# Two dense layers in split float32 on TensorE: the moving operand read as two halves in turn, one column of each

## The reference

```python
proj = h @ w_in                      # 2048 x 13312 of block one, 2048 x 6160 of block two
oa @ w_o_attn; orr @ w_o_ret; merged @ w_out
g, u = jnp.split(h2 @ w_ffn_in, 2, axis=-1)      # 2048 x 11264
x + (jax.nn.silu(g) * u) @ w_ffn_out             # 5632 x 2048
```

## Time and profile before

| | |
|---|---|
| median of 3 runs | 2798.41 us (2797.48 to 2807.46) |
| the profiled execution, its own time | 2805.7 us |
| its span | 2803.6 us |
| granted TensorE clock, mean | 0.995 |
| busy: TensorE / VectorE / ScalarE / GpSimd | 2757.4 / 1602.8 / 1309.6 / 89.6 us |
| HBM read | 504.39 MB, mean 181 GB/s |

### The profile page before, as it was taken

One profiled execution on the slowest core, in us unless ns is written; L12 is line 12 of the kernel. 1 busy time (PEld: TensorE's weight loads), 2 busy tenths in 40 slices (PEclk: granted clock), 3 DMA queues, 4 the chain that ended last, 5 costly groups with the idle time before them and its releaser, 6 DMA issues.

```text
span 2803.6 us, 37336 instructions
## 1 busy us (share of the span) xinstructions
PE 2757.4 (98%) x13344; PEld 2302.9 (82%) x13344; DVE 1602.8 (57%) x1640; ACT 1309.6 (47%) x1545; POOL 89.6 (3%) x61
## 2 busy tenths in 40 slices
PE   8999999999999999999999999998999999999998
PEld 7887778788888888888888888787788888888886
DVE  5557655545555444444454555586676666666455
ACT  5445555454445444444444444454554444444444
POOL 0000000000000000000000000021000000000000
PEclk9999999999999999999999999999999999999999
DMA  7665555566666666666666666543456666666554
GB/s 233 184 184 164 160 170 163 166 207 213 188 188 182 193 187 187 188 188 192 187 193 192 189 180 184 154 128 121 143 173 191 190 188 187 188 191 192 193 193 150
DMA packets 233286, 507.67 MB, mean 181 GB/s; under 512 B 15829, under 2 KB 18229, under 8 KB 232436
## 3 DMA queue, kind: packets, MB, share of 16 engines
q1 hardware_dynamic: 231712, 499.31, 59.6%
q0 software_dynamic: 1360, 7.21, 0.8%
q10 hardware_dynamic: 132, 0.03, 0.0%
HBM read 504.39 MB, written 2.10 MB: 181 GB/s over the span
## 4 chain that ended last, share of the span: by engine, by line
PE 94%; DVE 2%; ACT 2%; issue 1%; DMA 0%; DVEq 0%; ACTq 0%; SPq 0%
PE ps L359 20%; PE ps L361 20%; PE ps L360 20%; PE ps L349 18%; PE ps L350 10%; DVE wlo L1303 1%; PE ps L426 1%; ACT whi L841 1%; PE ps L730 1%; PE ps L722 0%; PE ps L663 0%; ACT hT L887 0%; PE ps L494 0%; PE ps L784 0%; PE ps L557 0%
## 5 line engine op out<-in xcount | busy, mean ns | idle before, releaser
L1303 DVE TENSOR_TENSOR wlo<-raw,whi 128x1024 fp32r<-128x1024 f32 x944 | 1172.3, 1243 | 1123.2 <-ACT whi L841 1115.2
L841 ACT ACTIVATE whi<-raw 128x1024 fp32r<-128x1024 f32 x944 | 999.9, 1060 | 1418.5 <-PE ps L361 991.3
L349 PE MATMUL ps<-hT,whi 128*128 128x512 f32 x2304 | 807.7, 395 | 5.8 <-DVE wlo L1303 4.2
L359 PE MATMUL ps<-whi,hT 128*128 128x512 f32 x1792 | 715.4, 399 | 7.5 <-ACT big L945 2.4
L361 PE MATMUL ps<-whi,hT 128*128 128x512 f32 x1792 | 701.7, 392 | 0.0
L360 PE MATMUL ps<-wlo,hT 128*128 128x512 f32 x1792 | 701.0, 391 | 0.0
L350 PE MATMUL ps<-hT,wlo 128*128 128x256 f32 x2304 | 645.7, 280 | 0.0
L349 PEld LDWEIGHTS ps<-hT,whi 128*128 128x128 f32 x2304 | 431.7, 187 | 106.6 <-issue 4.8
L350 PEld LDWEIGHTS ps<-hT,wlo 128*128 128x128 f32 x2304 | 435.4, 189 | 0.1
L359 PEld LDWEIGHTS ps<-whi,hT 128*128 128x128 f32 x1792 | 338.5, 189 | 80.3 <-issue 2.9
L361 PEld LDWEIGHTS ps<-whi,hT 128*128 128x128 f32 x1792 | 338.3, 189 | 71.9
(11 more groups left out here) (246 smaller groups left out, 1084.6 us busy)
## 6 DMA issues: line engine op xcount, KB each, us to landing
raw<-w_ffn_in SPq DMA_DIRECT2D x352, 512.0 KB, 3.7
raw<-w_in SPq DMA_DIRECT2D x304, 512.0 KB, 3.8
raw<-w_ffn_out SPq DMA_DIRECT2D x176, 512.0 KB, 3.6
raw<-w_o_ret SPq DMA_DIRECT2D x32, 512.0 KB, 4.7
raw<-w_out SPq DMA_DIRECT2D x32, 512.0 KB, 3.9
raw<-w_o SPq DMA_DIRECT2D x32, 512.0 KB, 3.6
raw<-w_o_attn SPq DMA_DIRECT2D x16, 512.0 KB, 4.3
resid<-x SPq DMA_DIRECT2D x8, 256.0 KB, 6.2
```

Source lines behind the costliest of these rows:

```text
L349: pe.matmul(acc, whi[:, c % SLOTS, f], hT[:, kt, :, :], start=(kt == 0), stop=False)
L359: pe.matmul(acc, hi, whi[:, c % SLOTS, f], start=start, stop=False)
L841: act.activation(whi[:, c % SLOTS, :], raw[:, c % SLOTS, :], ACT.Copy).then_inc(hi_ready, 1)
L1303: dve.tensor_tensor(wlo[:, c % SLOTS, :], raw[:, c % SLOTS, :], whi[:, c % SLOTS, :].bitcast(F32), ALU.subtract).then_inc(lo_ready, 1)
```

## The change

The numbers that are computed stay the same; only the order of columns inside a bank changes. A new helper `in_turn` reads a run of N columns as two halves of N/2 and takes one column of each in turn: 0, N/2, 1, N/2 + 1, and so on. The weight products (`cols_block` and `rows_mm`) take their moving operand in that order, so the sums lie in PSUM in that order. The matmuls still write PSUM in order. Stationary operands, the small float32 matmuls and the transposes are as before.

Every reader of those accumulators now reads PSUM in order (`as_taken` only gives the same addresses the shape of the other operand) and reads and writes its SBUF operands through `in_turn`. In `rows_mm` and in the `rows` readers the two halves of 512 columns lie 256 columns (1024 bytes) apart. In `cols_block` each 256-column part is halved by itself, so the two lie 128 columns (512 bytes) apart. No instruction, wait, buffer or transfer is added or removed.

```diff
+        def in_turn(x):
+
+            return x.rearrange("p (b a) -> p a b", b=2) if len(x.shape) == 2 else x.rearrange("p n (b a) -> p n a b", b=2)
+
+        def as_taken(acc):
+
+            return acc.rearrange("p (a b) -> p a b", b=2) if len(acc.shape) == 2 else acc.rearrange("p n (a b) -> p n a b", b=2)
...
-                            pe.matmul(acc, whi[:, c % SLOTS, f], hT[:, kt, :, :], start=(kt == 0), stop=False)
-                            mm = pe.matmul(acc[:, 0:SEQ], wlo[:, c % SLOTS, f], hT[:, kt, 0, :], start=False,
+                            pe.matmul(acc, whi[:, c % SLOTS, f], in_turn(hT[:, kt, :, :]), start=(kt == 0), stop=False)
+                            mm = pe.matmul(acc[:, 0:SEQ], wlo[:, c % SLOTS, f], in_turn(hT[:, kt, 0, :]), start=False,
                                            stop=(kt == KT - 1))
...
-                pe.matmul(acc, hi, whi[:, c % SLOTS, f], start=start, stop=False)
-                pe.matmul(acc, hi, wlo[:, c % SLOTS, f], start=False, stop=False)
-                return pe.matmul(acc, lo, whi[:, c % SLOTS, f], start=False, stop=stop)
+                w_hi, w_lo = in_turn(whi[:, c % SLOTS, f]), in_turn(wlo[:, c % SLOTS, f])
+                pe.matmul(acc, hi, w_hi, start=start, stop=False)
+                pe.matmul(acc, hi, w_lo, start=False, stop=False)
+                return pe.matmul(acc, lo, w_hi, start=False, stop=stop)
...
-                act.activation(lo_sum.rearrange("p (f t) -> p f t", f=4), ps[:, 4 * par:4 * par + 4, SEQ:], ACT.Copy)\
+                act.activation(in_turn(lo_sum.rearrange("p (f t) -> p f t", f=4)),
+                               as_taken(ps[:, 4 * par:4 * par + 4, SEQ:]), ACT.Copy)\
                     .then_inc(lo_copied, 1)
...
-                return dve.tensor_tensor(dst, ps[:, 4 * par:4 * par + 4, 0:SEQ], lo_sum.rearrange("p (f t) -> p f t", f=4), ALU.add)
+                return dve.tensor_tensor(in_turn(dst), as_taken(ps[:, 4 * par:4 * par + 4, 0:SEQ]),
+                                         in_turn(lo_sum.rearrange("p (f t) -> p f t", f=4)), ALU.add)
...
-                        ins = dve.scalar_tensor_tensor(hid_rows[:, t, :], ps[:, 2 + t, :], late[:, t:t + 1], gate_rows[:, t, :],
-                                                       ALU.mult, ALU.mult)
+                        ins = dve.scalar_tensor_tensor(in_turn(hid_rows[:, t, :]), as_taken(ps[:, 2 + t, :]), late[:, t:t + 1],
+                                                       in_turn(gate_rows[:, t, :]), ALU.mult, ALU.mult)
...
-                return dve.tensor_tensor(rows_a[:, t, q * 512:q * 512 + 512], ps[:, 2 * q + t, :], area_g[:, q * 512:q * 512 + 512], ALU.mult)
+                return dve.tensor_tensor(in_turn(rows_a[:, t, q * 512:q * 512 + 512]), as_taken(ps[:, 2 * q + t, :]),
+                                         in_turn(area_g[:, q * 512:q * 512 + 512]), ALU.mult)
```

More of the change, by code:

```diff
@@ L944, in epilogue @@
                     for t in range(NT):
-                        ins = act.activation(dst[:, t, bass.ds(i * 512, 512)], ps[:, 2 * par + t, :], func, scale=late[:, t:t + 1])
+                        ins = act.activation(in_turn(dst[:, t, bass.ds(i * 512, 512)]), as_taken(ps[:, 2 * par + t, :]), func,
+                                             scale=late[:, t:t + 1])
                     ins.then_inc(acc_freed, 1)
@@ L1061, in pair @@
                     for t in range(NT):
-                        ins = act.activation(gate_rows[:, t, :], ps[:, t, :], ACT.Silu, scale=late[:, t:t + 1])
+                        ins = act.activation(in_turn(gate_rows[:, t, :]), as_taken(ps[:, t, :]), ACT.Silu, scale=late[:, t:t + 1])
                     ins.then_inc(acc_freed, 1)
@@ L1536, in times_silu @@
                 dve.wait_ge(S("silu"), i + 1)
-                o = resid[:, :, bass.ds(i * 512, 512)]
-                dve.tensor_tensor(o, o, ps[:, 2 * par:2 * par + 2, :], ALU.mult).then_inc(acc_freed, 1)
+                o = in_turn(resid[:, :, bass.ds(i * 512, 512)])
+                dve.tensor_tensor(o, o, as_taken(ps[:, 2 * par:2 * par + 2, :]), ALU.mult).then_inc(acc_freed, 1)
             dve.wait_ge(S("r_done"), R_HEADS)
@@ L1570, in _ @@
                 cs = slice(n * 512, n * 512 + 512)
-                own(dve.tensor_tensor(rows_a[:, :, cs], rows_a[:, :, cs], ps[:, 2 * par:2 * par + 2, :], ALU.mult))
+                r = in_turn(rows_a[:, :, cs])
+                own(dve.tensor_tensor(r, r, as_taken(ps[:, 2 * par:2 * par + 2, :]), ALU.mult))
                 own(dve.tensor_tensor(rows_d[:, :, cs], rows_d[:, :, cs], rows_a[:, :, cs], ALU.add))
@@ L1592, in _ @@
                 dve.wait_ge(S("x_again"), 16)
-                r = resid[:, :, n * 512:n * 512 + 512]
-                own(dve.tensor_tensor(r, r, ps[:, 2 * par:2 * par + 2, :], ALU.add))
+                r = in_turn(resid[:, :, n * 512:n * 512 + 512])
+                own(dve.tensor_tensor(r, r, as_taken(ps[:, 2 * par:2 * par + 2, :]), ALU.add))
                 dve.sem_inc(acc_freed, 1)
@@ L1672, in add_resid @@
                     for t in range(NT):
-                        r = resid[:, t, q * 512:q * 512 + 512]
-                        ins = dve.tensor_tensor(r, r, ps[:, 2 * q + t, :], ALU.add)
+                        r = in_turn(resid[:, t, q * 512:q * 512 + 512])
+                        ins = dve.tensor_tensor(r, r, as_taken(ps[:, 2 * q + t, :]), ALU.add)
                     own(ins)
@@ L1831, in keep_m @@
                 if n >= 2:
-                    m = rows_m[:, :, cs]
-                    dve.tensor_tensor(m, m, ps[:, bank + 2 * hc:bank + 2 * hc + 2, :], ALU.add).then_inc(S("norm_in7"), 1)
+                    m = in_turn(rows_m[:, :, cs])
+                    dve.tensor_tensor(m, m, as_taken(ps[:, bank + 2 * hc:bank + 2 * hc + 2, :]), ALU.add).then_inc(S("norm_in7"), 1)
                 else:
-                    dve.tensor_copy(rows_m[:, 1, cs], ps[:, bank + 2 * hc + 1, :]).then_inc(S("m_kept1"), 1)
+                    dve.tensor_copy(in_turn(rows_m[:, 1, cs]), as_taken(ps[:, bank + 2 * hc + 1, :])).then_inc(S("m_kept1"), 1)
             for n in range(4):
@@ L1856, in _ @@
                             block_done(blk)
-                        m = rows_m[:, t, 1536:2048]
-                        dve.tensor_tensor(m, m, ps[:, 6 + t, :], ALU.add).then_inc(S("norm_in7"), 1)
+                        m = in_turn(rows_m[:, t, 1536:2048])
+                        dve.tensor_tensor(m, m, as_taken(ps[:, 6 + t, :]), ALU.add).then_inc(S("norm_in7"), 1)
                     dve.wait_ge(S("norm_in7"), 5)
@@ L1921, in out_gain @@
                 dve.wait_ge(S("norm_part"), 4 * NORMS.index(8) + q + 1)
-                own(dve.tensor_tensor(rows_a[:, :, q * 512:q * 512 + 512], ps[:, 2 * q:2 * q + 2, :], row_gain(q), ALU.mult))
+                own(dve.tensor_tensor(in_turn(rows_a[:, :, q * 512:q * 512 + 512]), as_taken(ps[:, 2 * q:2 * q + 2, :]),
+                                      in_turn(row_gain(q)), ALU.mult))
             def out_gains(k):
```

4 lines of the change are left out of this document (2 added, 2 removed).

## The result

The changed kernel takes 2688.66 us (median of 4 runs, 2687.57 to 2689.59). The kernel before, run beside it, takes 2802.93 us (4 runs, 2797.48 to 2809.44). The ratio is 0.9591 with an interval of 0.9565 to 0.9617: 4.1% faster. The forecast of 2660 us and the range of 2630 to 2850 us had the sign and the size, but the gain is some 25 us smaller than forecast. The profiled execution takes 2689.59 us, its span is 2687.5 us, 116.1 us shorter than before.

A forecast was written before the change was run, and what follows sets the result against it. TensorE, busy 98%, was taken as the bound: matmul count times start distance. 2805.7 - 140 + 1 = 2667 us; the same steps from the median 2798.4 give 2659, stated as 2660, range 2630 to 2850 us.

The forecast's parts named there:

- The surplus: TensorE weight matmuls: 13.3 ns each beyond their columns, 166 us in all, laid to the supply of the moving operand.
- If the reader keeps two places open: TensorE's moving reads: two runs of addresses give two fetches that don't wait for each other, leaving 0.8 ns over.
- rival two: Weight matmuls, L349 to L361: TensorE reads at half rate, +2250 us, 5050 us in all; chance 0.19.
- part one: Order of the moving reads in the weight matmuls: 12.5 ns less for each of 12480, nine tenths taken, -140 us.
- pairs 320 to 325 ns apart: Sign in the profile after: cols-form pairs L349 and L350 start this far apart, where 346.7 ns was taken before.
- The discount to nine tenths: Weight matmuls: late starts after waits or stage changes and lower-clock stretches cut -156 us to -140 us.
- Part two: Readers of the accumulators, SBUF side alternating: only those on the chain are bare, 0 to +5 us, +1 taken.
- the other view: Readers' SBUF operands: alternation costs what VectorE's stepped reduction pays, 794 ns per 1024 elements and operand.
- the high price: Readers at the stepped reduction's cost: L863 and L1340 grow to 1.8 and up to 2.8 us; with scaling 6.6 us.
- Cover: Loops: idle waits of 1115 us on VectorE and 1413 us on ScalarE hide longer readers; TensorE waits at block heads would refute it.
- part three: Faster TensorE: splitters' busy shares rise by 6%, DMA goes from 195 to 207 GB/s, nothing becomes the bound.
- the readers pay, TensorE doesn't gain: L863, L1340 at their high price, with waits at some block heads: +5 to +45 us, 2803 to 2845; chance 0.09.

The follow-up runs named there:

- e1_pe_alone: Against the changed kernel, only the matmuls read in turn; readers are those of the kernel before, so columns come out in another order; 2672.59 us, ratio 0.9516.
- e8: Against the changed kernel, readers take PSUM with a step of two columns and SBUF in order; 2672.92 us, ratio 0.9546 to the kernel before.
- e7: The changed kernel once more, nothing altered, on the same chip as e8; 2688.57 us, ratio 0.9600 to the kernel before.
- e2_readers_alone: Against the changed kernel, matmuls read in order, readers still in turn, so columns come out in another order; 2822.32 us, ratio 1.0043 to the kernel before.

## Why the prediction was right, and where not

**The surplus was the moving operand's supply: right.** The distance was forecast at 214 to 216 ns and is 215.8. In the streams only the order of the moving operand changed and the surplus went with it, and the same stationary operand did not remove it. Whether the fetch is too slow by itself or because each matmul's weight load runs beside it, no run tells.

**Why this order cures it: the picture was wrong.** "If the reader keeps two places open" fell, by the column read twice and by halves each read twice. The argument gave the right answer for two halves, and would have given it for pairs (328 ns) and quarters (283 ns) too, which are losses. So the mechanism behind the largest term was wrong, and that the sign came out right for this order was luck. The half rate (rival two) is also real, at a step of two columns (453 ns); the order decides it, and of its neighbours pairs, fours, eights and quarters all lose.

Of the rule in the Trainium skill's SBUF — State Buffer (Specifications (TRN2)), 16-byte lines with two hits wanted and a penalty at each crossing, part is borne out: distances fall into steps that go by how much of 16 bytes is used at a time. But every access of the change crosses to another line and it is faster than in order, and in order, with four hits, is not the full rate for float32r. The measurement decides.

**The size of part one: nearly right.** -140 us were forecast, -130 counted and -132.4 measured (e1_pe_alone). Forecast was a remaining surplus of 0.8 ns; it is 2.5 in the rows form and (327.5 - 320) / 2 = 3.7 ns in the cols form. There the sign of pairs 320 to 325 ns apart was missed: 327.5 is 215.8 + 111.7, and 111.7 ns is what a matmul of 128 columns takes too, so the 256 columns meet a limit that the prediction did not have. The discount to nine tenths was for late starts, and they exist: TensorE is idle for 52.0 us in e1_pe_alone and was for 46.2 before, 5.8 us more. Its busy time fell by 138.2 us, more than the 130 counted, in part because the pairs of the cols stages up to 1800 us had taken 353 ns and not the 346.7 counted with; that makes 50 us and not 44 from that form.

**Part two failed.** "I take +1, since the same argument as above holds for them." It does not: on ScalarE and VectorE the write in turn costs 686 to 942 ns for 1024 elements, and measured is +15.6 us (e8 against e7) or +12 (e2_readers_alone, some 4 of them not the readers'), beyond the +5 given as the upper bound. The sign "wrong if L1340 reads 2.0 us or more" came: it reads 2.08. The price of an element, up to 794 ns for 1024, was in the text as the other view and would have been near for one reader, but not for the term: the +5 is already made with it. Two things were missing. The argument for +1 was about a read, while these are writes, which no row of before showed. And the earlier trace rows gave the readers on the chain before; with double durations others join it, such as L872 at 188.28 us, and TensorE then waits some 10 us more and is longer at the lower clock. A slip without consequence: at the high price L863, L1340 and the scaling need 1.80 + 2.81 + 1.23 = 5.8 us, not 6.6.

The Trainium skill's Vector Engine (DVE) Microarchitecture Reference (§5.2 Measured stream behaviour on trn2) has the write too: 1.71 ns an element for a destination that hops 4 KiB each element against 1.05. By this page I estimate 0.67 us more for 1024 elements; here, with hops of 512 bytes, VectorE showed 0.69. Its exception for one alternating read was the sentence I cited, and the row beside it was the one that applied. For a source that hops the page has 1.73 ns in a two-source operation; here, with the other source in PSUM, it is free (1194 ns), so that price does not carry over.

**Cover and part three: right in the loops.** Splits rose to 68.51 and 58.53 of 130 us where the prediction had 6% more, DMA to 204 GB/s, and nothing was bound by them; the 36 cols blocks hid the long readers. The sign against the cover, waits of TensorE for VectorE "at the heads of blocks", came true only at handovers of stages.

**The sum.** Forecast was 2660 / 2798.4 = 0.9506, measured 0.9591, 24 us apart. The readers are 14.6 of it (15.6 - 1), the distance 7.6 (140 - 132.4); 2 us are within the scatter of runs. The other 4.5 us between 2660 and 2688.66 are the kernel before itself, 2802.93 us in this comparison.

The rival "the readers pay, TensorE doesn't gain" had its first half right. The forecast and that half were not exclusive, and I had priced them as if they were.

## What to carry to other kernels

When TensorE's stream of float32r matmuls of 512 columns runs at 226.7 ns, the order of its moving columns is worth 5% of the stream: two halves in turn, one column of each, or another of the orders that measured 215.8 ns above. Measure the exact order, since neighbours of it cost 7 to 115% over reading in order. Undo the permutation where it is free: read PSUM with a step of two and leave the SBUF writes in order. And price a reader's operands one by one, reads apart from writes, then look at the handovers between stages, where no queue of other work covers them.

## What the runs showed of the hardware that was not expected

- The surplus belongs to a matmul, not to its length, down to where another limit takes over: in order and in turn are 120.0 and 111.7 ns for 256 columns, 173.3 and 162.5 for 384; for 128 columns they are 111.6 and 111.7, so the 256 columns in turn stand at that limit already.
- In order, but starting one column (4 bytes) off a 16-byte boundary, costs 236.7 ns, two columns off 233.3, where an aligned start has 226.7. Halves in turn hardly mind (216.6).
- bf16 in order has no surplus (215.8 ns), and loses more than half its rate in turn (484 ns).
- A plain float32 matmul leaves two records: 24 of them stand as x48 in the rows of L82 above, 429 ns each. So L722 in the earlier trace rows is two matmuls of 857 ns, not four of 428. The prediction took a record for a matmul; its argument, that there is no surplus at half the demand, does not hang on it.
- Whether a matmul could write its columns to PSUM in a stepped order, and spare the readers altogether, wasn't tried.
